# Odd layer of a two-block network: head scores as three fp32r products, and another spacing of the heads

## The chip, the cores and the metric

The kernel runs on one core of a Trainium2 chip. The metric is the device time of one execution in microseconds (us), median of several runs. Engines: PE is TensorE's matmul, PEld its weight load, DVE is VectorE, ACT is ScalarE, POOL is GpSimd, SP is SyncE.

## The reference, cut to what matters

Two blocks follow each other. The first has an even layer and an odd layer; the change touches the odd layer's mixer alone, an mLSTM with 8 heads over 256 latent and 256 context tokens. In short, for each head `h` and each direction `d` (causal and anti-causal):

```
D[q, k]  = i[k] + cum[q] - cum[k]           masked by the direction
mu[q]    = max_k D[q, k]
W_d[q,k] = (Q[q] . K[k]) / sqrt(128) * exp(D[q, k] - mu[q])
den[q]   = max(|sum_k W_d[q, k]|, exp(-mu[q] ...))
out[q]   = sum over d of (W_d / den) V ,  then gated, normalised per head, scaled
```

`Q` has 256 rows of 128 channels, `K` 512, `V` 512 rows of 256 channels. The normalisation of a head divides by the square root of the mean square of its 256 outputs. The outputs of all heads then go through the output weights.

## The kernel before

**How work is ordered.** Each engine runs one fixed instruction stream per layer. Every piece of work is a small generator that yields a due time, in an abstract unit, before each of its steps; `merge` takes the steps of all generators of an engine in the order of their due times (at equal due times in the order in which the stages are listed: `dense`, `heads`, `norm`, `turn`, `out`, and the weight feed last). So a due time does not start anything: it sets the place of an instruction in its engine's queue, and an instruction that waits holds up all behind it. ScalarE's table loads are put by the compiler in front of an ACTIVATE whose function the loaded table lacks.

**The stream of weights.** One unit of due time is 12 split matmuls of line 182 (`split_matmul`: lead x lead, lead x rest, rest x lead, each 128x512). The odd layer's input projection is four items of 16 units: v (units 16i to 16i+8, in four steps of 2), o (four steps of 1) and z (four steps of 1). In v a group of six matmuls is due every 0.5, in o and z too. For a step due at `u`, ACT takes the lead of the weights three steps ahead at `u + 0.02` (L343, after PE has finished the step before `u`), DVE takes the rest at `u + 0.3` (L155), and SP starts a load at `u + 0.5`. The output projection is units 64 to 80. The outputs of the groups are read by ACT: o with Sigmoid (L2634) at 16i+11.6 and 16i+12.1, z with Silu (L2624) at 16i+15.6 and 16i+16.1, v by ACT and DVE in turn (copies, L2616 and L2617).

**The heads.** Head `h` has a start `S`. Its steps and their due times, with `t` = 0, 1 the two blocks of 128 queries and `d` = 0, 1 the directions:

| engine | step (line) | due |
|---|---|---|
| DVE | maxima: decay tile and its row maximum (L2450, L2452) | S + 0.25 + d + 0.4t |
| ACT | decays: Exp of the tile, Exp of the floor (L2459, L2461) | S + 0.6 + d + 0.4t |
| PE | score (L2472) | S + 1.2 + 3t |
| DVE | mix: both directions times the score, sums, reciprocals (L2483 to L2492) | S + 2.2 + 3t |
| PE | four transposes of the mixed tile (L2503), wait for the mix | S + 3.6 + 3t |
| ACT | copy of the transposed tile (L2512) | S + 3.9 + 3t |
| PE | values (L2522) | S + 4.3 + 3t |
| DVE | gate (L2533) | S + 4.7 + 3t |
| ACT | Square with a sum (L2542) | S + 5.0 + 3t |
| DVE | gain times z, even heads (L2571) | S + 7.6 |
| DVE | mean (L2579), waits for the squares | S + 8.6 |
| ACT | Sqrt (L2587), waits for the mean | S + 8.7 |
| DVE | reciprocal and two scales (L2595, L2599), wait for the Sqrt | S + 9.1 |

The starts are 11.7, 17.7, 27.7, 33.7, 43.7, 49.7, 59.7 and 65.7. Behind the heads, `Turn` transposes the finished outputs of head `n` on PE (L783, one PSUM bank, so each waits for DVE's L2660 of the one before), ACT takes their lead (L2659) 0.3 later and DVE their rest (L2660) 0.6 later. The score is one fp32 matmul of 128x512, which the trace shows as two PE records. The keys `kT` and queries `qT` are fp32.

Of the kernel before, what the change touches and what calls it, by code (L numbers as in the profile page):

```python
# [7 lines left out]
ALU = mybir.AluOpType  # L8
# [5 lines left out]
P = 128  # L14
# [61 lines left out]
class Core:  # L76


    def __init__(self, nc, a, ctx):
        self.nc, self.a, self.ctx = nc, a, ctx  # L80
        sb = lambda name, shape: ctx.enter_context(nc.sbuf_tensor(name, shape, F32))
        with ExitStack() as c:
            low = lambda name, n, kind: c.enter_context(nc.sbuf_tensor(name, [P, n], kind))
            low("under_x", 2560, F32)
            first = low("q_lead0", BANK, F32R)
            low("under_ga", LEAD_GAP, F32)
            self.query_leads = (low("q_lead1", BANK, F32R), first)
        self.x = sb("x_res", [P, NT, D])
        self.hT = sb("hT", [P, KC, 2 * SEQ])
        self.ring = sb("weights", [P, Stream.RAW, 2048])  # L90
        self.cols = sb("cols", [P, NCOL])
        self.ident = sb("ident", [P, P])
        self.ga = sb("ga", [P, 3, D])
        self.mod = sb("mod", [P, 2, 2, KC, 2])
        self.gate = self.ga[:, 2, 0:72]
        self.gate_rows = nc.dram_tensor("gate_spread", (3 * KC, P), F32).ap()
        self.small = sb("small", [P, 256])
        self.ps = ctx.enter_context(nc.psum_tensor("psum", [P, 8, BANK], F32))
        keep = lambda name: ctx.enter_context(nc.semaphore(name))

        self.tables_in, self.tables_n = keep("tables_in"), 0
        self.stored = keep("result_stored")
        self.dve_chain = Chain(keep("dve_step"))
        self.act_chain = Chain(keep("act_step"))
        self.pool_chain = Chain(keep("pool_step"))
        self.stream = Stream(self, keep)
        self.fresh, self.old = ([], ExitStack()), ([], ExitStack())
# [293 lines left out]
class Feed(Stage):  # L401
# [19 lines left out]
    def leads(self, act):  # L421
        for i, at in self.ahead():
            yield at + self.offsets[0] + self.leads_later.get(i, 0.0)
            self.core.stream.take_lead(act, i)
# [4 lines left out]
    def rests(self, dve):  # L429
        if self.before:  # L430
            yield -2.0
            self.core.stream.take_rest(dve, self.before.last_split())
        for i, at in list(self.ahead())[:-1 if self.defer else None]:
            yield at + self.offsets[1] + self.rests_later.get(i, 0.0)
            self.core.stream.take_rest(dve, i)
# [1803 lines left out]
class OddRoom:  # L2239
    def __init__(self, core):  # L2240
        nc = core.nc
        sb = lambda s, name, shape: s.enter_context(nc.sbuf_tensor("o_" + name, shape, F32))
        with ExitStack() as c:
            v1 = sb(c, "v1", [P, NT, 2 * ML_V])
            with ExitStack() as early:
                self.v = (sb(early, "v0", [P, NT, 2 * ML_V]), v1)
                self.kT = sb(early, "kT", [P, ML_H, 2 * SEQ])
                self.h = Split(nc, early, "o_h", [P, KC, 2 * SEQ])
                self.o_gate = sb(early, "o", [P, LT, ML_H * ML_V])
                with ExitStack() as gates:  # L2250
                    self.wg = Split(nc, gates, "o_wg", [P, KC, P])
                self.Dm = sb(early, "decay", [P, LT, 2, 2 * SEQ])
                self.WT = sb(early, "WT", [P, LT, 2 * SEQ])
                self.spread = sb(early, "spread", [P, 2, 2 * SEQ])
            hs_first = c.enter_context(nc.sbuf_tensor("o_hs_first", [P, 8, SEQ], F32R))
            self.hsT = Split(nc, c, "o_hsT", [P, 16, SEQ])
        flat = core.hT[:].rearrange("p k t -> p (k t)")
        self.z = flat[:, 0:2048].rearrange("p (i t n) -> p i t n", i=2, t=LT)
        self.out_src = HeadFeatures(self.hsT, hs_first)
        self.gain = flat[:, 2048:3072].rearrange("p (i n) -> p i n", i=2)  # L2260
        self.scratch, self.wg32 = flat[0:40, 0:3072].rearrange("p (n t) -> p n t", n=6), flat[:, 3072:3712]
        self.junk = flat[:, 3712:3968]
        self.qT = core.ga[:, 0:2, :].rearrange("p a (b t) -> p (a b) t", t=SEQ)
        spare = core.x[:, LT:NT, :].rearrange("p t d -> p (t d)")
        self.masks = spare[:, 0:(2 * LT + 1) * SEQ].rearrange("p (n t) -> p n t", n=2 * LT + 1)
        self.aT = spare[0:40, 1280:1280 + 2 * SEQ]
        self.cumT = spare[:, 1792:1792 + LT * 40].rearrange("p (t r) -> p t r", t=LT)
        self.a_rows = nc.dram_tensor("gate_rows", (40, 2 * SEQ), F32).ap()
        self.mu, self.nmu, self.flr, self.den, self.rec = (core.small[:, 96 + 32 * i:128 + 32 * i] for i in range(5))
        self.ssq, self.root, self.norm = (core.small[:, 16 * i:16 * i + 16] for i in range(3))  # L2270
# [130 lines left out]
class Mlstm(Stage):  # L2401
# [3 lines left out]
    def __init__(self, core, odd, gates, dense, taps_done, banks, starts, step):  # L2405
        self.core, self.odd, self.gates, self.dense, self.taps_done, self.banks, self.starts, self.step = core, odd, gates, dense, taps_done, banks, starts, step
        s = lambda n: core.sem("ml_" + n)
        self.spread_in = [core.lasting(f"spread_in{i}") for i in range(2)]
        self.negmax, self.decayed, self.floored, self.scored = s("negmax"), s("decayed"), s("floored"), s("scored")
        self.mixed, self.turned, self.WT_ready, self.valued, self.out_done, self.squared = s("mixed"), s("turned"), s("WT_ready"), s("valued"), s("out_done"), s("squared")  # L2410
        self.tensor = (self.scores, self.turns, self.values)
        self.vector, self.scalar, self.gpsimd = (self.maxima, self.mixes, self.outs), (self.decays, self.copies, self.squares), (self.spreads,)

    def logs(self):

# [38 lines left out]
    def decays(self, act):  # L2454
        nc, odd = self.core.nc, self.odd
        for u, h, d, t, at in self.logs():
            yield at + 0.6
            act.wait_ge(self.negmax, u + 1)
            nc.scalar.activation(odd.Dm[:, t, d, :], odd.Dm[:, t, d, :], ACT.Exp, bias=odd.nmu[:, u:u + 1]).then_inc(self.decayed, 1)  # L2459
            r = 32 * d + h  # L2460
            nc.scalar.activation(odd.flr[:, u:u + 1], odd.cumT[:, t, r:r + 1], ACT.Exp, bias=odd.nmu[:, u:u + 1], scale=-1.0).then_inc(self.floored, 1)  # L2461

    def scores(self, pe):
        nc, ps, odd = self.core.nc, self.core.ps, self.odd
        for j, h, t, at in self.jobs(1.2):
            yield at
            if j == 0:
                pe.wait_ge(self.taps_done, 4)
                pe.wait_ge(self.gates.done, 1)
            else:  # L2470
                pe.wait_ge(self.mixed, j)
            nc.tensor.matmul(ps[:, self.banks[1], :], odd.qT[:, h, t * P:(t + 1) * P], odd.kT[:, h, :], start=True, stop=True).then_inc(self.scored, 1)  # L2472

    def mixes(self, dve):
        nc, ps, odd, link = self.core.nc, self.core.ps, self.odd, self.core.dve_chain
        for j, h, t, at in self.jobs(2.2):
            yield at
            dve.wait_ge(self.scored, j + 1)
            for d in range(2):
                u = 4 * h + 2 * d + t  # L2480
                c = slice(u, u + 1)
                dve.wait_ge(self.decayed, u + 1)
                link(dve, nc.vector.tensor_tensor_reduce(odd.Dm[:, t, d, :], ps[:, self.banks[1], :], odd.Dm[:, t, d, :],  # L2483
                                                         ML_QK ** -0.5, 0.0, ALU.mult, ALU.add, odd.den[:, c]))
            dve.wait_ge(self.floored, 4 * h + 2 + t + 1)
            both = lambda z: z[:, 4 * h + t:4 * h + t + 3:2]
            link(dve, nc.vector.scalar_tensor_tensor(out=both(odd.rec), in0=both(odd.den), scalar=-1.0, in1=both(odd.den), op0=ALU.mult, op1=ALU.max))
            link(dve, nc.vector.tensor_tensor(both(odd.den), both(odd.rec), both(odd.flr), ALU.max))
# [114 lines left out]
def odd_layer(core, odd):  # L2603
# [2 lines left out]
    keys_left = LeftOuts(core, "o_qk_left_", odd.qk, -4.0, 0.3)  # L2606
    gates.keys_out = keys_left.wait
    tokens = lambda n: [("tokens", t, 0, BANK) for t in range(n)]
    starts = [11.7 + 16 * (h // 2) + 6.0 * (h % 2) for h in range(ML_H)]
    taps_done = core.sem("taps_done")  # L2610

    def v_out(i, g):
# [41 lines left out]
    def turn_ready(pe, n):  # L2654
        pe.wait_ge(norm.scaled, 2 * n + 2)
        if n < 4:
            pe.wait_ge(heads.valued, 12)
    turn = Turn(core, "od_t_", blocks, [57.0, 58.2, 59.4, 60.6, 63.2, 63.9, 70.0, 76.0], (5,),
                act=lambda n: lambda act, src: nc.scalar.activation(hsT.lead(n), src, ACT.Copy),  # L2659
                dve=lambda n: lambda dve, src: nc.vector.tensor_tensor(hsT.rest(n), src, hsT.lead(n).bitcast(F32), ALU.subtract),  # L2660
                ready=turn_ready)
# [16 lines left out]
class OddEnd:  # L2678
# [5 lines left out]
    def tables_free(self, pool):  # L2684

        pool.wait_ge(self.heads.scored, LT * ML_H)
        pool.wait_ge(self.heads.floored, 2 * LT * ML_H)
        pool.wait_ge(self.heads.negmax, 2 * LT * ML_H)

    def x_ready(self, eng, k=KC - 1, t=LT - 1):  # L2690
# [969 lines left out]
```

## Time and profile before

| | |
|---|---|
| median of 3 runs | 1777.19 us (1777.16 to 1777.56) |
| profiled execution, its own time | 1777.32 us |
| its span in the trace | 1775.5 us |
| mean granted clock | 0.998 of full speed |
| PE busy | 1725.6 us (97%) |
| DVE busy | 1170.9 us (66%) |
| ACT busy | 917.4 us (52%) |
| odd layer's heads in the trace | about 664 to 890 us |

The span is what the trace holds from the first to the last instruction; the device time is 1.8 us longer in this execution. A matmul's end is modelled, so the cost of a matmul is read from one start to the next, not from its duration. In a timeline row the number in brackets is the engine's idle time before it, and what ended it.

### The profile page before, as it was taken

The numbers are of one execution on the slowest core, as the hardware profiler recorded it, in microseconds if no ns is written. First come the engines' busy times: TensorE is split into PE (matmuls) and PEld (weight loads), VectorE is DVE, ScalarE is ACT, GpSimd is POOL, SyncE is SP. The second block draws the span as 40 slices with busy tenths as digits, with TensorE's granted clock in tenths as the row PEclk, the third lists the DMA queues.
The fourth block names the chain that finished last, engine by engine and source line by source line (L and its number), as shares of the span: only waits on it lengthen the run. The fifth ranks groups of instructions, "written<-read, shape, count | busy, mean of one in ns | idle before, by whom it ended". The sixth has DMA issues, their size and how long they took to land. (4 is left out here: it accounts for less than half of the span.)

```text
span 1775.5 us, 22881 instructions
## 1 busy us (share of the span) xinstructions
PE 1725.6 (97%) x8547; PEld 1392.6 (78%) x8547; DVE 1170.9 (66%) x2154; ACT 917.4 (52%) x1497; POOL 49.5 (3%) x68
## 2 busy tenths in 40 slices
PE   8999999999998999999999999999999999999998
PEld 3866888777787777777778787788887787878886
DVE  6654566688438467766767775777646867577744
ACT  4332554433326355656656556467534746547743
POOL 0000000000000000000100002000000002000000
PEclk9999999999999999999999999999999999999999
DMA  9466221221325444453544444556555454555562
GB/s 344 152 207 214 96 72 48 72 72 56 134 95 191 138 125 127 149 154 110 164 154 149 143 155 166 171 182 193 190 190 159 137 165 142 184 165 178 190 217 74
DMA packets 115974, 267.24 MB, mean 151 GB/s; under 512 B 5413, under 2 KB 9838, under 8 KB 115673
## 3 DMA queue, kind: packets, MB, share of 16 engines
q1 hardware_dynamic: 111384, 252.26, 43.5%
q0 software_dynamic: 3504, 10.96, 2.1%
q10 hardware_dynamic: 976, 2.57, 0.4%
q8 instruction: 68, 1.11, 0.3%
q14 instruction: 42, 0.34, 0.1%
HBM read 264.63 MB, written 1.14 MB: 150 GB/s over the span
## 5 line engine op out<-in xcount | busy, mean ns | idle before, releaser
L155 DVE TENSOR_TENSOR qw_rest<-weights,qw_lead 128x1024 fp32r<-128x1024 f32 (+2 forms) x428 | 519.9, 1221 | 373.4 <-ACT qw_lead L343 368.1
L343 ACT ACTIVATE qw_lead<-weights 128x1024 fp32r<-128x1024 f32 (+2 forms) x428 | 446.2, 1048 | 454.1 <-PE psum L182 412.9
L182 PE MATMUL psum<-qw_lead,b_h_pair 128*128 128x512 f32 (+1 forms) x960 | 319.7, 398 | 4.0 <-ACT b_gates L3003 1.3
L182 PEld LDWEIGHTS psum<-qw_lead,b_h_pair 128*128 128x128 f32 x960 | 180.3, 188 | 44.7 <-issue 3.7
L182 PE MATMUL psum<-qw_rest,b_h_pair 128*128 128x512 f32 (+1 forms) x480 | 186.2, 388 | 0.0
L175 PE MATMUL psum<-b_h_pair,qw_lead 128*128 128x512 f32 x512 | 178.1, 393 | 2.0 <-DVE b_h_pair L722 2.0
L176 PE MATMUL psum<-b_h_pair,qw_rest 128*128 128x256 f32 x512 | 142.6, 279 | 0.0
L182 PE MATMUL psum<-e_h_lead,qw_lead 128*128 128x512 f32 x320 | 132.0, 413 | 2.2 <-DVE e_qT L1599 1.4
L182 PE MATMUL psum<-e_h_lead,qw_rest 128*128 128x512 f32 x320 | 125.7, 393 | 0.0
L182 PE MATMUL psum<-e_h_rest,qw_lead 128*128 128x512 f32 x320 | 125.0, 391 | 0.0
L175 PEld LDWEIGHTS psum<-b_h_pair,qw_lead 128*128 128x128 f32 x512 | 95.9, 187 | 24.3 <-DVE b_h_pair L722 2.8
L182 PE MATMUL psum<-qw_lead,o_h_lead 128*128 128x512 f32 x256 | 108.8, 425 | 0.3 <-PEq L129 0.3
L182 PEld LDWEIGHTS psum<-qw_rest,b_h_pair 128*128 128x128 f32 x480 | 90.4, 188 | 14.9
L182 PE MATMUL psum<-qw_lead,o_h_rest 128*128 128x512 f32 x256 | 100.0, 391 | 0.0
L182 PE MATMUL psum<-qw_rest,o_h_lead 128*128 128x512 f32 x256 | 99.9, 390 | 0.0
L182 PE MATMUL psum<-qw_lead,b_upT_rest 128*128 128x512 f32 x256 | 99.6, 389 | 0.0
L182 PE MATMUL psum<-qw_rest,b_upT_lead 128*128 128x512 f32 x256 | 99.6, 389 | 0.0
L182 PE MATMUL psum<-qw_lead,b_upT_lead 128*128 128x512 f32 x256 | 99.6, 389 | 0.0
L176 PEld LDWEIGHTS psum<-b_h_pair,qw_rest 128*128 128x128 f32 x512 | 96.5, 188 | 0.0
L182 PE MATMUL psum<-qw_lead,e_h_lead 128*128 128x512 f32 x224 | 88.6, 396 | 1.1 <-DVE e_qT L2149 1.1
L182 PE MATMUL psum<-qw_lead,e_h_rest 128*128 128x512 f32 x224 | 87.3, 390 | 0.0
L182 PE MATMUL psum<-qw_rest,e_h_lead 128*128 128x512 f32 x224 | 87.2, 389 | 0.0
(490 smaller groups left out, 3033.5 us busy)
## 6 DMA issues: line engine op xcount, KB each, us to landing
weights<-in_w_in SPq DMA_DIRECT2D x48, 1024.0 KB, 5.1
weights<-in_o_w_in SPq DMA_DIRECT2D x32, 1024.0 KB, 5.4
weights<-in_w_mlp_up SPq DMA_DIRECT2D x32, 1024.0 KB, 5.5
weights<-in_w_mlp_down SPq DMA_DIRECT2D x32, 1024.0 KB, 4.9
weights<-in_e_w_in SPq DMA_DIRECT2D x26, 1024.0 KB, 5.1
weights<-in_w_mod SPq DMA_DIRECT2D x24, 1024.0 KB, 7.2
weights<-in_e_w_out SPq DMA_DIRECT2D x8, 1024.0 KB, 5.0
weights<-in_o_w_out SPq DMA_DIRECT2D x8, 1024.0 KB, 4.9
```

What stands on the lines that cost most here:

```text
L155: return eng.tensor_tensor(self.rest[at], src, self.lead[at].bitcast(F32), ALU.subtract)
L175: nc.tensor.matmul(out, lhs[0], pair, start=start, stop=False)
L176: return nc.tensor.matmul(out[:, 0:lead.shape[1]], lhs[1], lead, start=False, stop=stop)
L182: mm = nc.tensor.matmul(out, l, r, start=start and i == 0, stop=stop and i == 2)
L343: self.core.nc.scalar.activation(self.buf.lead[self.at(u)], self.raw(u), ACT.Copy).then_inc(self.lead_ready, 1)
```

## The change

The score becomes three fp32r products of split heads, as everywhere else in the kernel. For that each head's `kT` (128x512) and `qT` (128x256) are split: ACT writes their leads (`leads`, due S - 0.95) and DVE subtracts them (`rests`, due S - 0.7), in place over `kT` and `qT`. PE waits for them at the score. The two semaphores of the decays become one. The starts become 11.7 + 7.7h (11.7, 19.4, 27.1, 34.8, 42.5, 50.2, 57.9, 65.6), and the first two output transposes are due 57.8 and 58.6 in place of 57.0 and 58.2. All other due times keep their distance from `S`.

```diff
+        with ExitStack() as c:
+            c.enter_context(nc.sbuf_tensor("under_hT", [P, 3072], F32))
+            self.odd_head_lead = c.enter_context(nc.sbuf_tensor("o_head_lead", [P, 3 * SEQ], F32R))
...
+            self.odd_q_rest = c.enter_context(nc.sbuf_tensor("o_q_rest", [P, ML_H, SEQ], F32R))
...
+                    self.k_rest = rests.enter_context(nc.sbuf_tensor("o_k_rest", [P, ML_H, 2 * SEQ], F32R))
...
-        self.junk = flat[:, 3712:3968]
+        self.junk = flat[:, 3840:4096]
+        self.k_lead, self.q_lead, self.q_rest = core.odd_head_lead[:, 0:2 * SEQ], core.odd_head_lead[:, 2 * SEQ:3 * SEQ], core.odd_q_rest
...
+        self.vector, self.scalar, self.gpsimd = (self.rests, self.maxima, self.mixes, self.outs), (self.leads, self.decays, self.copies, self.squares), (self.spreads,)
+
+    def leads(self, act):
+        odd = self.odd
+        for h in range(ML_H):
+            yield self.starts[h] - 0.95
+            if h:
+                act.wait_ge(self.scored, LT * h)
+                act.wait_ge(self.lead_then_rest, 4 * h)
+            else:
+                act.wait_ge(self.taps_done, 4)
+                act.wait_ge(self.gates.split, 4)
+            self.core.nc.scalar.activation(odd.k_lead, odd.kT[:, h, :], ACT.Copy).then_inc(self.lead_then_rest, 1)
+            self.core.nc.scalar.activation(odd.q_lead, odd.qT[:, h, :], ACT.Copy).then_inc(self.lead_then_rest, 1)
+
+    def rests(self, dve):
+        odd = self.odd
+        for h in range(ML_H):
+            yield self.starts[h] - 0.7
+            for rest, whole, lead in ((odd.k_rest, odd.kT, odd.k_lead), (odd.q_rest, odd.qT, odd.q_lead)):
+                dve.wait_ge(self.lead_then_rest, 4 * h + 2)
+                self.core.nc.vector.tensor_tensor(rest[:, h, :], whole[:, h, :], lead.bitcast(F32), ALU.subtract).then_inc(self.lead_then_rest, 1)
...
-            nc.tensor.matmul(ps[:, self.banks[1], :], odd.qT[:, h, t * P:(t + 1) * P], odd.kT[:, h, :], start=True, stop=True).then_inc(self.scored, 1)
+            if t == 0:
+                pe.wait_ge(self.lead_then_rest, 4 * h + 4)
+            qs = slice(t * P, (t + 1) * P)
+            split_matmul(nc, ps[:, self.banks[1], :], (odd.q_lead[:, qs], odd.q_rest[:, h, qs]), (odd.k_lead, odd.k_rest[:, h, :]), True, True).then_inc(self.scored, 1)
...
-                dve.wait_ge(self.decayed, u + 1)
+                dve.wait_ge(self.decay_then_floor, 2 * u + 1)
...
-            dve.wait_ge(self.floored, 4 * h + 2 + t + 1)
+            dve.wait_ge(self.decay_then_floor, 2 * (4 * h + 2 + t + 1))
...
-    starts = [11.7 + 16 * (h // 2) + 6.0 * (h % 2) for h in range(ML_H)]
+    starts = [11.7 + 7.7 * h for h in range(ML_H)]
...
-    turn = Turn(core, "od_t_", blocks, [57.0, 58.2, 59.4, 60.6, 63.2, 63.9, 70.0, 76.0], (5,),
+    turn = Turn(core, "od_t_", blocks, [57.8, 58.6, 59.4, 60.6, 63.2, 63.9, 70.0, 76.0], (5,),
```

## Rows read from the trace of the kernel before

**Rows 1.** The page: busy time, share of the span, instructions.

```profile
PE 1725.6 (97%) x8547; PEld 1392.6 (78%) x8547; DVE 1170.9 (66%) x2154; ACT 917.4 (52%) x1497; POOL 49.5 (3%) x68
```

**Rows 2.** Busy time of each engine in 30 us of the heads; last three: granted clock, DMA share, GB/s.

```profile
665.00:695.00 30.00, 29.26 (x128) 23.07 (x127) 22.47 (x56) 20.59 (x35) 2.68 (x5) 1.00 0.53 159
```

**Rows 3.** Waits of PE between 630 and 915 us: total, times, longest.

```profile
PE psum L2503 <- DVE o_decay L2492: 2.4, 4, 0.7
```

**Rows 4.** Timeline of PE around the first score.

```profile
666.82 1.02 PE L2472 MATMUL psum<-o_kT,ga 128*128 128x512 f32 x2
...
667.91 0.40 PE L182 MATMUL psum<-qw_rest,o_h_lead 128*128 128x512 f32 x1
```

**Rows 5.** Timeline of PE: the first head's transposes, then its values, then transposes unhindered.

```profile
674.30 0.39 PE L182 MATMUL psum<-qw_lead,o_h_rest 128*128 128x512 f32 x1
675.42 0.66 PE L2503 MATMUL psum<-ident,o_decay 128*128 128x128 f32 x4 [0.74 <-DVE o_decay L2492]
...
690.82 1.89 PE L2522 MATMUL psum<-o_v,o_WT 128*128 128x256 f32 x8
...
692.78 0.39 PE L182 MATMUL psum<-qw_rest,o_h_lead 128*128 128x512 f32 x1
...
698.00 0.60 PE L2503 MATMUL psum<-ident,o_decay 128*128 128x128 f32 x4
...
698.67 0.40 PE L182 MATMUL psum<-qw_rest,o_h_lead 128*128 128x512 f32 x1
```

**Rows 6.** Timeline of PE, late waits of the stage.

```profile
848.43 0.66 PE L2503 MATMUL psum<-ident,o_decay 128*128 128x128 f32 x4 [0.20 <-DVE o_decay L2492]
851.39 0.63 PE L783 MATMUL psum<-ident,o_o 128*128 128x128 f32 x4 [0.91 <-DVE o_hsT_rest L2660]
```

**Rows 7.** Timeline of ACT up to and through the first head's decays.

```profile
661.63 1.06 ACT L343 ACTIVATE qw_lead<-weights 128x1024 fp32r<-128x1024 f32 x1 [1.66 <-PE psum L182]
...
664.51 1.05 ACT L343 ACTIVATE qw_lead<-weights 128x1024 fp32r<-128x1024 f32 x1
665.45 0.59 ACT L2634 ACTIVATE o_o<-psum 128x512 f32<-128x512 f32 x1
666.06 1.28 ACT L2459 ACT_TABLE_LOAD   x1
667.35 0.72 ACT L2459 ACTIVATE o_decay<-o_decay,small 128x512 f32<-128x512 f32 x1
...
668.17 0.71 ACT L2459 ACTIVATE o_decay<-o_decay,small 128x512 f32<-128x512 f32 x1
```

**Rows 8.** Timeline of DVE: the first head's last maximum and mix.

```profile
671.19 0.68 DVE L2450 CUSTOM_DVE_ANT_0 o_decay<-o_spread,x_res 128x512 f32<-128x512 f32 x1
...
672.03 0.69 DVE L2483 CUSTOM_DVE_ANT_0 o_decay<-psum,o_decay 128x512 f32<-128x512 f32 x1
...
672.77 0.69 DVE L2483 CUSTOM_DVE_ANT_0 o_decay<-psum,o_decay 128x512 f32<-128x512 f32 x1
...
675.28 2.35 DVE L155 TENSOR_TENSOR qw_rest<-weights,qw_lead 128x1024 fp32r<-128x1024 f32 x2
```

**Rows 9.** Timeline of ACT: Exp's table loaded again behind a Sqrt, in a later layer.

```profile
960.72 1.28 ACT L3118 ACT_TABLE_LOAD   x1
...
963.21 1.28 ACT L2784 ACT_TABLE_LOAD   x1
```

**Rows 10.** Groups by line, 640 to 910 us: count, busy us, mean ns, idle before.

```profile
L2459 ACT ACT_TABLE_LOAD x8 | 10.3, 1283 | 0.1
L2599 DVE SCALAR_TENSOR_TENSOR o_o<-o_o,small,hT 128x256 f32<-128x256 f32 x16 | 7.0, 481 | 0.3
L2542 ACT ACTIVATE hT<-o_o 128x256 f32<-128x256 f32 x16 | 6.7, 416 | 22.9 <-DVE o_o L2533 22.9
...
L2587 ACT ACT_TABLE_LOAD x4 | 5.1, 1283 | 0.1
...
L2659 ACT ACTIVATE o_hsT_lead<-psum 128x512 fp32r<-128x512 f32 x8 | 4.7, 592 | 5.0 <-PE psum L783 5.0
```

More of the change, by code:

```diff
@@ L92, in __init__ @@
         self.ident = sb("ident", [P, P])
+        with ExitStack() as c:
+            self.odd_q_rest = c.enter_context(nc.sbuf_tensor("o_q_rest", [P, ML_H, SEQ], F32R))
         self.ga = sb("ga", [P, 3, D])
@@ L2246, in __init__ @@
                 self.v = (sb(early, "v0", [P, NT, 2 * ML_V]), v1)
+                with ExitStack() as rests:
+                    self.k_rest = rests.enter_context(nc.sbuf_tensor("o_k_rest", [P, ML_H, 2 * SEQ], F32R))
                 self.kT = sb(early, "kT", [P, ML_H, 2 * SEQ])
@@ L2408, in __init__ @@
         self.spread_in = [core.lasting(f"spread_in{i}") for i in range(2)]
-        self.negmax, self.decayed, self.floored, self.scored = s("negmax"), s("decayed"), s("floored"), s("scored")
+        self.negmax, self.decay_then_floor, self.lead_then_rest, self.scored = s("negmax"), s("decay_then_floor"), s("lead_then_rest"), s("scored")
         self.mixed, self.turned, self.WT_ready, self.valued, self.out_done, self.squared = s("mixed"), s("turned"), s("WT_ready"), s("valued"), s("out_done"), s("squared")
         self.tensor = (self.scores, self.turns, self.values)
-        self.vector, self.scalar, self.gpsimd = (self.maxima, self.mixes, self.outs), (self.decays, self.copies, self.squares), (self.spreads,)
+        self.vector, self.scalar, self.gpsimd = (self.rests, self.maxima, self.mixes, self.outs), (self.leads, self.decays, self.copies, self.squares), (self.spreads,)
[18 more added lines that the diff above has]
+                self.core.nc.vector.tensor_tensor(rest[:, h, :], whole[:, h, :], lead.bitcast(F32), ALU.subtract).then_inc(self.lead_then_rest, 1)
     def logs(self):
@@ L2458, in decays @@
             act.wait_ge(self.negmax, u + 1)
-            nc.scalar.activation(odd.Dm[:, t, d, :], odd.Dm[:, t, d, :], ACT.Exp, bias=odd.nmu[:, u:u + 1]).then_inc(self.decayed, 1)
+            nc.scalar.activation(odd.Dm[:, t, d, :], odd.Dm[:, t, d, :], ACT.Exp, bias=odd.nmu[:, u:u + 1]).then_inc(self.decay_then_floor, 1)
             r = 32 * d + h
-            nc.scalar.activation(odd.flr[:, u:u + 1], odd.cumT[:, t, r:r + 1], ACT.Exp, bias=odd.nmu[:, u:u + 1], scale=-1.0).then_inc(self.floored, 1)
+            nc.scalar.activation(odd.flr[:, u:u + 1], odd.cumT[:, t, r:r + 1], ACT.Exp, bias=odd.nmu[:, u:u + 1], scale=-1.0).then_inc(self.decay_then_floor, 1)
     def scores(self, pe):
@@ L2467, in scores @@
             if j == 0:
-                pe.wait_ge(self.taps_done, 4)
                 pe.wait_ge(self.gates.done, 1)
@@ L2686, in tables_free @@
         pool.wait_ge(self.heads.scored, LT * ML_H)
-        pool.wait_ge(self.heads.floored, 2 * LT * ML_H)
+        pool.wait_ge(self.heads.decay_then_floor, 4 * LT * ML_H)
         pool.wait_ge(self.heads.negmax, 2 * LT * ML_H)
```

## The prediction

> **What bounds the kernel now.** I read the page first: PE is busy 97% of the span [rows 1], and in 30 us of the heads it works 29.3 us at the full granted clock while DVE works 22.5 and ACT 20.6 [rows 2]. So the layer costs what PE's queue costs plus the places where PE waits. Next the waits of PE from 630 to 915 us: the only one that repeats is the head's transposes (L2503) waiting for DVE's mix, four times, 2.4 us by the records [rows 3]. Then the timeline of PE, because ends are modelled there and only starts can be trusted. Between 692.78 and 698.00 there are 23 split matmuls, 0.227 us each [rows 5]. A group of six is therefore 1.36 us, a unit of due time 2.72. By starts the first head's transposes begin 675.42 and could have begun 674.30 + 0.23 = 674.53: 0.9 us lost, and so in the first head of the second and third pair. The fourth loses 0.4 at 848.43, L783 at 851.39 loses 1.1, having waited for L2660 of the transposes before it [rows 6], and one of its kind 0.2: 4.4 us in all. Last the timelines of ACT and DVE before the first mix, to see what made it late: ACT loads a table and works off Sigmoid, Exp and the weight lead in turn [rows 7], and DVE's last maximum, ahead of the mix in its queue, stands behind a weight rest that waited for such a lead [rows 8]. The feed of split weights itself never holds PE up for long. That is the reader's picture: PE has no slack, and between a head's score and its transposes lie 2.4 units in which ACT and DVE must get through.
>
> **What PE saves.** A score goes from 666.82 to 667.91 - 0.23, so 0.86 us [rows 4]. Three split products of the same shape cost 3 x 0.227 = 0.68. For 16 scores that is 16 x 0.18 = 2.9 us. Both bounds: the three could cost more where they meet other work, the first matmul behind transposes starting late (698.67 against 698.00 makes transposes cost 0.44, [rows 5]), but the score has split matmuls before and behind it nearly everywhere, so I take 2.9, with 0 as the other end.
>
> **What is added.** The trace has no split of a head. Nearest are the fp32r copy of 128x512, 0.59, and an ACTIVATE of 128x256, 0.42 [rows 10], so about 1.0 us of ACT for each head and, since L155 takes 1.17 for 1024 columns [rows 8], about 1.1 of DVE. They are due 2.1 units (5.8 us) ahead of the score. For the first head they fall where ACT has 1.66 us idle [rows 7]; I price them at nothing there. Without such cover they delay the decays by up to 1.0 a head, which I count for the last head alone, where the gains precede them.
>
> **What the spacing moves.** This is the larger part. A head's Sqrt is due S + 8.7. With starts 7.7 apart that is the next head's S + 1.0, the very due time of its second Exp, with two more Exp behind. Before, the next start was S + 6 or S + 10, and the Sqrt fell behind all four Exp or ahead of them. A Sqrt between Exps needs a table load before and after it: the trace shows Exp's table loaded again right behind Sqrt's at 963.21 [rows 9], 1.28 us each. Beside it, the Trainium skill (ScalarE: Activation LUTs, section "Table sets: the hidden batching unit") says that calls should be batched by set, all Exps and then all Sqrts, since the two lie in different sets; this change does the opposite. The same page (section "What ACT_TABLE_LOAD costs") gives about 2.66 us for each switch with a drain; here Exp starts 1.29 after its load began and the load began as the Sigmoid ended, so the trace does not agree, and by that figure each load below would cost 1.4 more. Also, the Sigmoids of o (16i + 11.6, 16i + 12.1) no longer precede the Exps of heads 2, 4 and 6 but fall among them.
>
> By the due times head 2 gets: Sigmoid 27.6, Exp 27.7, weight lead 28.02, Sigmoid 28.1, Exp 28.1, Sqrt 28.1, Exp 28.7. That is six table loads where the first head of a pair had two. Counting the whole stage, about 13 loads are added, 16.7 us of ACT. The prices: load 1.29, Exp with floor 0.82, weight lead 0.94, Sigmoid 0.6 (starts in [rows 7]), Square with its read 0.5 and Sqrt 0.2 (a little above [rows 10] and from the same timeline as [rows 9]), mix 3.25 of which 2.51 after its second operand, from DVE to PE 0.14 [rows 5, 8]. From PE to ACT I take 0.2.
>
> Head 2, from the end of the values of head 1 (PE at 27.0): 0.2 + 0.94 + Square 0.5 + (1.29 + 0.6) + (1.29 + 0.82) + 0.94 + (1.29 + 0.6) + (1.29 + 0.82) + Sqrt (1.29 + 0.2) + (1.29 + 0.72) + mix 2.51 + 0.14 = 16.7 us. PE in that time has four units and a score, 4 x 2.72 + 0.68 = 11.6. It waits 5.2 us.
>
> Head 4 starts with Exp's table loaded: from 43.0, 0.2 + 0.94 + 0.82 + 0.82 + Sqrt 1.49 + Sigmoid 1.89 + 0.94 + 0.6 + 2.01 + 2.51 + 0.14 = 12.4 against seven groups and a score, 10.2: 2.2 us.
>
> Head 5, from the values' end at 50: 0.2 + 0.94 + 0.5 + 1.29 + 0.82 + 0.82 + 1.49 + 2.11 + lead 0.94 + rest 1.17 (due 52.3, just ahead of the mix at 52.4) + 3.25 + 0.14 = 13.7 against eight groups and a score, 11.6: 2.1 us. Heads 1 and 3 have the same Exp, Sqrt, Exp. There DVE's scales wait for the Sqrt and the last maximum stands behind them: for head 1, gate 0.6, Square 0.5, 2.11, lead 0.94, 0.82, 1.49, scales 1.0 (two of 0.48, [rows 10]), maximum 0.84, 3.25, 0.14 = 11.7, so 0.1 lost; for head 3 a rest more but less waiting for ACT, 11.9, so 0.3.
>
> Head 6: its Exps share ACT with Sqrt, both Sigmoids and the copies of the output transposes. The third copy, due 59.7, stands behind Exp, copy, Exp, Sqrt, lead, Exp and Sigmoid. From 58.0 it ends at 12.0 us, its rest on DVE at 12.7; PE reaches the fourth output transposes (60.6) at 10.0: 2.7 us. Behind it 0.4 at the values of head 6, whose copy follows the second Sigmoid, and 1.2 at the transposes due 63.9, where 1.1 was lost before. Head 7: the gains hold DVE until 1.6 after the values, then Square, lead, 2.11, 0.82, 1.49, lead, scales, maximum, rest and mix: 14.0 against 11.6, 2.4 us. Head 0 keeps its old order and its old mix time, but PE arrives 0.18 earlier: 1.1.
>
> **The sum.** Waits after: 1.1 + 0.1 + 5.2 + 0.3 + 2.2 + 2.1 + 2.7 + 0.4 + 1.2 + 2.4 = 17.7 us; before: 4.4. Less 2.9 for the scores: 17.7 - 4.4 - 2.9 = 10.4 us more. The profiled execution took 1777.3 us (span 1775.5), 0.1 above the median, so I predict 1787.7 us. Nothing after the heads changes its order: the last transposes stay at 76.0 and the output units at 64 to 80. The values (1.73, [rows 5]) and transposes cost what they did. No weight rest comes later than some 3 us before PE needs it, so the feed itself costs nothing.
>
> **Rivals.** (1) Faster: the even spacing does what even spacing should. For it speaks that ACT is idle a third of the time [rows 2] and that the mixes' waits came in the first heads of pairs only. If the table loads were covered, the waits beyond head 0's would go: -2.9 - 4.4 + 1.1 = -6.2, 1771. It decides if the 2.4 units (7.2 us with the score) suffice, that is if no head's ACT work runs beyond the 11.6 us window worked out above. Against it: head 2's loads alone are 7.7 us. Chance 0.14. (2) Nearly no change: heads 2 and 4 wait as computed, the others, computed within 3 us of their windows, do not: 7.4 + 1.1 + 1.1 (at 63.9) - 4.4 - 2.9 = +2.3, and a little more cover brings it within 0.2% (3.6 us): about 1779. Chance 0.12. (3) Dearer: queues fall so far behind that split weights arrive late too, or the clock falls when PE stands for 5 us. The rest due 29.3 ends about 18 us after 27.0 and PE needs it at 32, some 4.5 us later, after its own wait; five late rests of 1.2 us would add 6: 1794. PE's clock stood at 1.00 in every stretch I read, but no wait in them was as long. Chance 0.08. The forecast has 0.66. (4) That the change doesn't act: only if the scores cost 0.86 still; it takes 2.9 off the gain and leaves the sign.
>
> **Range and chances.** The low end joins rivals 1 and 2 at 1776, the high end 1794 is rival 3; about 1 in 10 lies below and less above. Forecast and rival 3, and a little of rival 2, are slower by over 0.2% (3.6 us, about what a measurement can tell): 0.77. Within 0.2%: 0.10. Faster: 0.13.
>
> **What would show it.** Right: some 33 table loads between 640 and 910 us in place of 20; PE waiting before the third head's transposes by about 5 us; L2503's waits for DVE the largest of PE's; three matmuls of 0.23 for a score. Wrong: L2503 without waits, or loads not placed between Exp and Sqrt. The likeliest error is the order at equal due times (28.1, 44.1), where another order of Sigmoid and Exp saves a load or two, and the 0.2 us steps that add up along ten instructions.

## The result, and the profile after

The changed kernel takes 1792.7 us (median of five, 1792.3 to 1798.2) against 1777.2 for the kernel before: ratio 1.0093, 95% interval 1.0080 to 1.0106, 15.6 us more. The profiled execution spans 1790.9 us, 15.4 more than before.

The page's line of busy times. PE and DVE have hardly more to do, ACT has 23 us more than its 917.4 in [rows 1]:

```profile
PE 1727.3 (96%) x8563; PEld 1400.0 (78%) x8563; DVE 1177.7 (66%) x2170; ACT 940.5 (53%) x1526; POOL 49.4 (3%) x68
```

Groups of ACT between 640 and 925 us, the table loads. There are 34 of them; before there were 21, with Exp's 8 and Sqrt's 4 in [rows 10]. L2488 is the Exp of the decays, L2618 the heads' Sqrt, L2665 the Sigmoid, L2655 the Silu. Line numbers are those of the changed kernel.

```profile
L2488 ACT ACT_TABLE_LOAD x15 | 19.2, 1283 | 0.3
L2618 ACT ACT_TABLE_LOAD x8 | 10.3, 1283 | 0.1
L2665 ACT ACT_TABLE_LOAD x6 | 7.7, 1283 | 0.1
L2655 ACT ACT_TABLE_LOAD x4 | 5.1, 1283 | 0.1
L2393 ACT ACT_TABLE_LOAD x1 | 1.3, 1283 | 0.0
```

Waits of PE from 630 to 930 us: engine, line, who it waited for, total, times, longest. The transposes' wait for the mix (L2534, L2503 before) went from 2.4 us in four to 14.3 in seven [rows 3]:

```profile
PE psum L2534 <- DVE o_decay L2523: 14.3, 7, 5.4
PE psum L788 <- DVE o_hs_first L2691: 2.8, 1, 2.8
PE psum L788 <- DVE o_hsT_rest L2691: 1.1, 1, 1.1
```

Timeline of PE at the first score: three matmuls from 665.42 to 666.11, 0.69 us in place of 0.86 [rows 4].

```profile
665.42 0.39 PE L187 MATMUL psum<-o_head_lead 128*128 128x512 f32 x1
665.65 0.39 PE L187 MATMUL psum<-o_k_rest,o_head_lead 128*128 128x512 f32 x1
665.88 0.40 PE L187 MATMUL psum<-o_head_lead,o_q_rest 128*128 128x512 f32 x1
666.11 0.40 PE L187 MATMUL psum<-qw_lead,o_h_lead 128*128 128x512 f32 x1
```

Timeline of ACT before the third head's mix. Read it from top to bottom: Sigmoid, Exp, weight lead, Sigmoid, Exp, Sqrt, Exp, each but the weight lead behind a load of 1.28, with no idle time between them.

```profile
718.08 1.28 ACT L2665 ACT_TABLE_LOAD   x1
719.38 0.60 ACT L2665 ACTIVATE o_o<-psum 128x512 f32<-128x512 f32 x1
720.00 1.28 ACT L2488 ACT_TABLE_LOAD   x1
...
722.10 1.05 ACT L348 ACTIVATE qw_lead<-weights 128x1024 fp32r<-128x1024 f32 x1
723.17 1.28 ACT L2665 ACT_TABLE_LOAD   x1
...
725.08 1.28 ACT L2488 ACT_TABLE_LOAD   x1
...
727.30 1.28 ACT L2618 ACT_TABLE_LOAD   x1
...
728.82 1.28 ACT L2488 ACT_TABLE_LOAD   x1
730.11 0.72 ACT L2488 ACTIVATE o_decay<-o_decay,small 128x512 f32<-128x512 f32 x1
```

Timeline of DVE in the same place: it stands 3.6 us at the reciprocal that waits for the Sqrt, with the last maximum and the mix queued behind it.

```profile
728.83 0.17 DVE L2626 RECIPROCAL small<-small 128x2 f32<-128x2 f32 x1 [3.62 <-ACT small L2618]
...
729.83 0.69 DVE L2479 CUSTOM_DVE_ANT_0 o_decay<-o_spread,x_res 128x512 f32<-128x512 f32 x1
...
730.68 0.69 DVE L2514 CUSTOM_DVE_ANT_0 o_decay<-psum,o_decay 128x512 f32<-128x512 f32 x1
...
733.27 0.75 DVE L2523 SCALAR_TENSOR_TENSOR o_decay<-o_decay,small 128x512 f32<-128x512 f32 x1
```

Timeline of PE there. It stands from 728.53 to 734.07, 5.5 us, and then the split matmuls come 0.43 apart, not 0.227, until 738.

```profile
728.30 0.39 PE L187 MATMUL psum<-qw_lead,o_h_rest 128*128 128x512 f32 x1
734.07 1.12 PE L2534 MATMUL psum<-ident,o_decay 128*128 128x128 f32 x4 [5.39 <-DVE o_decay L2523]
734.84 0.78 PE L187 MATMUL psum<-qw_lead,o_h_lead 128*128 128x512 f32 x1
735.41 0.63 PE L187 MATMUL psum<-qw_rest,o_h_lead 128*128 128x512 f32 x1
735.84 0.63 PE L187 MATMUL psum<-qw_lead,o_h_rest 128*128 128x512 f32 x1
...
738.34 0.40 PE L187 MATMUL psum<-o_head_lead,o_q_rest 128*128 128x512 f32 x1
```

Busy times in stretches; the third number from the end is the granted clock as a share of 2.4 GHz. It was partly at the lower level, 1.2 GHz, behind the wait.

```profile
700.00:730.00 30.00, 28.52 (x129) 23.08 (x127) 18.51 (x42) 20.77 (x29) 0.71 (x2) 1.00 0.45 137
730.00:735.00 5.00, 0.93 (x5) 0.93 (x6) 4.76 (x13) 3.70 (x7) 0.54 (x1) 0.64 0.17 52
735.00:740.00 5.00, 5.00 (x17) 4.09 (x17) 2.51 (x3) 3.42 (x4) 0.00 (x0) 0.67 0.53 141
```

**Where the 15.4 us are.** From the first score to the next layer's first matmul the trace of before takes 246.8 us (666.82 to 913.60), that of after 262.7 (665.42 to 928.15): 15.9 more. Ahead of it the execution before lost 1.4 us to a lower clock at 355 to 365 us that the one after did not have, behind it the one after lost 0.9. Within the stretch: waits counted by starts 19.6 against 4.4, +15.2; scores -2.9; matmuls at the lower clock after the waits at 734 (2.0) and 852 (1.3), +3.3. The clock was low at 926 too, on the last transposes of the stretch, but there it costs 0.1 only: they take 2.37 us to the next matmul against 2.27 before, because the kernel before waited for DVE in the same place, 0.5 us in all. That makes 15.7 for 15.9.

Timeline of PE at the end of the stretch, the kernel before:

```profile
911.33 1.09 PE L701 MATMUL psum<-ident,x_res 128*128 128x128 f32 x8 [0.61 <-DVE x_res L1889]
...
913.60 0.50 PE L182 MATMUL psum<-qw_lead,b_h_pair 128*128 128x512 f32 x1 [0.23 <-DVE b_h_pair L722]
```

The changed kernel:

```profile
925.78 2.45 PE L706 MATMUL psum<-ident,x_res 128*128 128x128 f32 x11 [0.61 <-DVE x_res L1894]
...
928.15 0.79 PE L187 MATMUL psum<-qw_lead,b_h_pair 128*128 128x512 f32 x1
```

### The profile page after: what moved, and what is told of

It is laid out like the page before. It is cut to its first block and busy times, and to the rows that moved or that the text cites. A ratio compares the mean times of both kernels' runs of the same rounds, so it can differ in the third digit from the quotient of the medians.

```text
span 1790.9 us, 22973 instructions
## 1 busy us (share of the span) xinstructions
PE 1727.3 (96%) x8563; PEld 1400.0 (78%) x8563; DVE 1177.7 (66%) x2170; ACT 940.5 (53%) x1526; POOL 49.4 (3%) x68
## 5 line engine op out<-in xcount | busy, mean ns | idle before, releaser
L160 DVE TENSOR_TENSOR qw_rest<-weights,qw_lead 128x1024 fp32r<-128x1024 f32 (+2 forms) x428 | 520.0, 1222 | 356.1 <-ACT qw_lead L348 350.8
L187 PE MATMUL psum<-qw_lead,o_h_lead 128*128 128x512 f32 x256 | 105.0, 410 | 0.3 <-PEq L134 0.3
```

The lines of the kernel that those rows point to most:

```text
L160: return eng.tensor_tensor(self.rest[at], src, self.lead[at].bitcast(F32), ALU.subtract)
L187: mm = nc.tensor.matmul(out, l, r, start=start and i == 0, stop=stop and i == 2)
```

## The experiments

The ratios are against the kernel before, run on the same chip in the same session; its median was between 1777.4 and 1778.2. "Stretch" is the time from the first score to the next layer's first matmul in the profiled execution, 246.8 us before and 262.7 after.

### The split alone

```diff
-    starts = [11.7 + 7.7 * h for h in range(ML_H)]
+    starts = [11.7 + 16 * (h // 2) + 6.0 * (h % 2) for h in range(ML_H)]
...
-    turn = Turn(core, "od_t_", blocks, [57.8, 58.6, 59.4, 60.6, 63.2, 63.9, 70.0, 76.0], (5,),
+    turn = Turn(core, "od_t_", blocks, [57.0, 58.2, 59.4, 60.6, 63.2, 63.9, 70.0, 76.0], (5,),
```

> The changed kernel with the old starts and the old output transposes: the split of the heads and the three products alone. If the order of ACT's queue is the cause, this gains what the scores save, 2.9 us, less 0.2 at each of the four or five places where PE already waited for a mix: 1774.5 to 1775.5, some 20 table loads between 640 and 910 us, no wait of PE over 1.3 us. If the added leads and rests (1.0 us of ACT and 1.1 of DVE a head) are the cause, it is slower than before, 1780 or more, and L2534's waits grow.

Measured 1777.1 us, ratio 0.9999 (0.9990 to 1.0008): no change, and less of a gain than either 2.9 or the 2 expected. Table loads are 21 again. Waits of PE in its trace, 630 to 900 us:

```profile
PE psum L2534 <- DVE o_decay L2523: 4.5, 4, 1.6
PE psum L788 <- DVE o_hsT_rest L2691: 0.9, 1, 0.9
```

The stretch is 246.3 us, 0.5 less. By starts the four waits at the mixes are 1.2, 1.1, 1.7 and 1.3, 5.3 us where the kernel before had 3.1: the scores' gain is spent on waiting, 0.18 a time because PE is earlier, and most of the rest because the leads and rests push the mix back at the fifth and seventh head. At the fifth ACT works without a break from the leads at 773.37 to the Exp at 779.90, so the leads' 0.8 us delay all behind them. The forecast had counted such a delay for the last head alone. The clock was low again from 910 to 915, but it costs nothing before the stretch ends: the last transposes take 2.28 us to the next matmul, 2.27 before. So the split doesn't cause the loss; nor does it gain.

### The spacing alone

```diff
-    starts = [11.7 + 16 * (h // 2) + 6.0 * (h % 2) for h in range(ML_H)]
+    starts = [11.7 + 7.7 * h for h in range(ML_H)]
...
-    turn = Turn(core, "od_t_", blocks, [57.0, 58.2, 59.4, 60.6, 63.2, 63.9, 70.0, 76.0], (5,),
+    turn = Turn(core, "od_t_", blocks, [57.8, 58.6, 59.4, 60.6, 63.2, 63.9, 70.0, 76.0], (5,),
```

> The kernel before with the even starts and the new output transposes: one fp32 score of 0.86 us, no split. If the order is the cause, it shows all the waits of the changed kernel, each 0.2 shorter since PE arrives later, and pays 2.9 for the scores: 1793 to 1795, 33 table loads, the third head's wait 5.3 us and the clock's fall behind it. If the split is the cause, 1777 to 1780.

Measured 1794.2 us, ratio 1.0088 (1.0075 to 1.0102), with the same 34 loads. Its waits of PE:

```profile
PE psum L2503 <- DVE o_decay L2492: 12.8, 6, 5.2
PE psum L783 <- DVE o_hs_first L2660: 2.6, 1, 2.6
PE psum L783 <- DVE o_hsT_rest L2660: 1.1, 1, 1.1
```

The third head's 5.2 us against 5.4 with the split, and the granted clock at 0.50 from 735 to 740 us behind it. This is what was expected if the order is the cause. The whole loss comes with the starts (the first two output transposes moved with them).

### Without the loads for the Sqrt

```diff
-            self.core.nc.scalar.activation(odd.root[:, c], odd.root[:, c], ACT.Sqrt).then_inc(self.rooted, 1)
+            self.core.nc.scalar.activation(odd.root[:, c], odd.root[:, c], ACT.Identity).then_inc(self.rooted, 1)
```

> The changed kernel with Identity in place of the heads' Sqrt (the head norms are not the reference's): the same instructions in the same order, without the table loads around the Sqrt. If the loads are the cause, the waits fall to about 1.2 (first head), 3.0 (third), 1.1 (fifth), 0.4 and 1.3 at the output transposes, 7 us in place of 19.6, and perhaps one slow stretch of PE is left: 1776 to 1779. If it is the place of the Sqrt in the queue (its wait for the mean, the scales waiting for it) or the spacing as such, 1789 to 1793.

Measured 1783.0 us, ratio 1.0025 (1.0016 to 1.0034), between the two ranges expected. The profiled execution was 1779.7, one of two with a mean granted clock of 0.999; the seven at 0.993 to 0.996 took 1782.7 to 1784.9. The stretch is 250.9 us, 11.8 less. Loads fall to 20 in the heads, the Ln's included. The direction is as expected, the size is not: at the third head 4.1 us by starts (4.0 by the record) are left, not 3.0.

```profile
PE psum L2534 <- DVE o_decay L2523: 7.2, 5, 4.0
PE psum L788 <- DVE o_hsT_rest L2691: 1.1, 1, 1.1
```

The timelines tell why: ACT's Identity starts at 726.70, but only behind the loads for Sigmoid and Exp ahead of it, and DVE's scales, last maximum and mix run off one after the other from there, so the load saved behind the Identity no longer counts.

```profile
726.92 0.17 DVE L2626 RECIPROCAL small<-small 128x2 f32<-128x2 f32 x1 [2.20 <-ACT small L2618]
...
728.77 0.69 DVE L2514 CUSTOM_DVE_ANT_0 o_decay<-psum,o_decay 128x512 f32<-128x512 f32 x1
```

### Without the loads for Sqrt and Sigmoid

```diff
-                          act=lambda g, cs=cs: lambda act, src: nc.scalar.activation(odd.o_gate[:, g, cs], src, ACT.Sigmoid)))
+                          act=lambda g, cs=cs: lambda act, src: nc.scalar.activation(odd.o_gate[:, g, cs], src, ACT.Identity)))
```

beside the edit of the run before.

> As the run with Identity for Sqrt, and Identity for the Sigmoid of the o gates too (neither is the reference's). If the loads are the cause, only the first head's wait and the one at the sixth output transposes stay, 2.5 us: 1771 to 1773, below the kernel before, with the granted clock at 1.00 throughout. If the even spacing itself or the split costs time, it stays above 1777.

Measured 1772.8 us, ratio 0.9974 (0.9963 to 0.9984), stretch 243.6. Even spacing, split, every instruction and every wait in its old place, and 10 loads in the heads: with the loads gone, the loss is gone. That is fewer than the 21 of the kernel before, so part of the gain over it is not the layout's. The waits are 3.2 us by the records and not 2.5, for the eighth head waits too.

```profile
PE psum L2534 <- DVE o_decay L2523: 2.1, 3, 1.1
PE psum L788 <- DVE o_hsT_rest L2691: 1.1, 1, 1.1
```

### The Sqrt behind the next head's Exps

```diff
-    norm = HeadNorm(core, odd, heads, dense, [at + 8.6 for at in starts])
+    norm = HeadNorm(core, odd, heads, dense, [at + (10.4 if h < ML_H - 1 else 8.6) for h, at in enumerate(starts)])
```

> The changed kernel, output as the reference's, with the head norms' mean, Sqrt and scales due 1.8 later for all but the last head, so behind the next head's four Exp. By the loads and the queue: third head 2.4, fifth 0.7, first 1.2, sixth output transposes 1.2, others nothing, 5.5 us in place of 19.6 and less of the slow clock: 1775 to 1778. If the even spacing costs by itself, above 1785.

Measured 1787.1 us, ratio 1.0050 (1.0034 to 1.0066): my size was wrong. The stretch is 254.5, 8.2 less than after. The third head waits 2.2 by starts, as expected, but the fifth still 2.3: I had forgotten that the moved Sqrt leaves its table loaded, so the fifth head's first Exp, which found its own before, must load one. 29 loads remain in the heads, the Ln's included. A wait of the values for ACT's copy is new:

```profile
PE psum L2534 <- DVE o_decay L2523: 7.1, 6, 2.1
PE psum L2553 <- ACT o_WT L2543: 1.8, 1, 1.8
PE psum L788 <- DVE o_hsT_rest L2691: 1.1, 1, 1.1
```

The eighth head waits 1.5. By its own words the expectation had read a time above 1785 as a cost of the even spacing by itself. The run before speaks against that reading: it has the same spacing without the loads and takes 1772.8.

The clock fell behind waits of 2.2 and 2.3 us:

```profile
730.00:735.00 5.00, 2.99 (x11) 2.26 (x10) 4.52 (x13) 4.22 (x7) 0.00 (x0) 0.77 0.54 156
...
790.00:795.00 5.00, 4.37 (x14) 3.65 (x15) 3.87 (x7) 3.34 (x5) 0.00 (x0) 0.66 0.25 94
```

### An even layout with the tables in order

```diff
-    starts = [11.7 + 7.7 * h for h in range(ML_H)]
+    starts = [11.7, 19.7, 27.7, 35.7, 43.7, 51.7, 59.7, 65.9]
...
-    norm = HeadNorm(core, odd, heads, dense, [at + 8.6 for at in starts])
+    norm = HeadNorm(core, odd, heads, dense, [at + (10.4 if h < ML_H - 2 else 8.6) for h, at in enumerate(starts)])
...
-    turn = Turn(core, "od_t_", blocks, [57.8, 58.6, 59.4, 60.6, 63.2, 63.9, 70.0, 76.0], (5,),
+    turn = Turn(core, "od_t_", blocks, [59.1, 60.0, 60.9, 61.8, 63.2, 63.9, 70.0, 76.0], (5,),
```

with the later transposes of the next run.

> Split, starts 8.0 apart (11.7 to 59.7, the last 65.9), norms behind the next head's Exps, the o gates' Sigmoids ahead of the Exps, first transposes 0.5 later, the first four output transposes moved behind the sixth head's values. Even layout without the interleaved tables: if the order on ACT was all, no wait over 0.5 us but the one at the output transposes due 63.9 (1.2 us), 1771 to 1773. If an even layout costs DVE or PE something else, 1776 or more.

Measured 1777.4 us, ratio 0.9999 (0.9990 to 1.0007), stretch 246.5. No mix is waited for any more, but the output transposes, closer together in the one bank, wait 3.2 us for DVE, and the values 2.0 for ACT's copy:

```profile
PE psum L788 <- DVE o_hs_first L2691: 3.2, 3, 2.1
PE psum L2553 <- ACT o_WT L2543: 2.0, 3, 0.7
```

So the second half of the expectation came true: this even layout costs something else, at the output transposes and at the copies, with 24 loads in the heads. An even layout needn't lose 15 us, but this one gains nothing over pairs.

### Later transposes, with the split and without

```diff
         for j, h, t, at in self.jobs(3.6):
-            yield at
+            yield at + (0.5 if t == 0 else 0.0)
...
         for j, h, t, at in self.jobs(3.9):
-            yield at
+            yield at + (0.3 if t == 0 else 0.0)
```

> Split and three products, old starts, and the transposes of each head's first block due 0.5 later (their copy 0.3). In the run with the split alone PE waited 1.2, 1.1, 1.7 and 1.3 us at those transposes. If these waits are where the scores' 2.9 us went, PE now does a group of split matmuls (1.36 us) in their place, some 5 us are gained and the time is 1772 to 1773.5. If PE's arrival was not what made them, or the later transposes delay the values, it stays at 1776 to 1778.

> The kernel before with the same later transposes and nothing else. PE waited 0.9, 0.9, 0.9 and 0.4 us there: 1774 to 1775.5. Beside the run with split and later transposes it shows what the three products are worth when no wait takes it back: 2.9 us if the price by starts is right, nothing if the split's work costs as much elsewhere.

Measured 1775.9 us with the split and the old starts (0.9987, 0.9978 to 0.9996), 1775.7 without the split (0.9984, 0.9975 to 0.9992). The waits at the mixes are gone but for 0.2. Without the split the expected gain is nearly there; with it, it fell short by 2 to 4 us, and the stretch is 244.1 against 243.9. Part of it went to the wait of the sixth output transposes for the rest of the fifth, 2.1 us by the record against 1.4:

```profile
PE psum L788 <- DVE o_hsT_rest L2691: 2.1, 1, 2.1
```

The clock was below full speed behind it, where the values take 2.6 us to the next matmul (849.02 to 851.64) in place of 1.5, and again at 905 to 915 us.

### And the sixth output transposes later

```diff
-    turn = Turn(core, "od_t_", blocks, [57.0, 58.2, 59.4, 60.6, 63.2, 63.9, 70.0, 76.0], (5,),
+    turn = Turn(core, "od_t_", blocks, [57.0, 58.2, 59.4, 60.6, 63.2, 65.1, 70.0, 76.0], (5,),
```

> The run with split, old starts and later transposes, and the sixth output transposes (due 63.9, where PE waited 2.4 us for DVE's rest of the fifth) due 65.1. If that wait is the last one in the heads' stretch, it goes, and the slow clock behind it: from the first score to the next layer's first matmul 241 us or less in place of 244.1, 1772 to 1774 in time. If the wait only moves to another transpose, 1775 to 1776.

> The same without the split, on the kernel before with later transposes, where that wait was 1.7 us: 1774 to 1775. The difference of the two stretches in the trace is what the three products are worth when nobody waits: 2.9 us if the price of 0.86 against 0.68 holds.

Measured 1774.1 us with the split (0.9978, 0.9968 to 0.9988) and 1774.0 without it (0.9974, 0.9964 to 0.9984). Both beat both kernels of this study. The stretches are 241.6 and 243.2: 1.6 us for the three products, not 2.9. By starts the trace with the split waits 1.4 us (0.4 for a mix, 1.1 for ACT's copy) against 0.7, so some 2.4 us come from PE's work itself. The clock was low at 905 to 910 with the split and full without, but up to the end of the stretch this costs nothing (the last transposes take 2.28 us in both). In the times nothing of the gain is seen.

```profile
PE psum L2553 <- ACT o_WT L2543: 0.9, 1, 0.9
PE psum L2534 <- DVE o_decay L2523: 0.2, 1, 0.2
```

## Why the prediction was right, and where it was off

The forecast was slower by 10.4 us, the kernel is slower by 15.6, inside the range.

**The order on ACT.** This held, for the third head instruction by instruction. Predicted were the six loads before the third head's mix and some 33 in place of 20 in the heads; the trace has 33, and one Ln load in both kernels. With the loads taken out of an otherwise unchanged queue the loss vanished, and with the starts alone it came whole. The Trainium skill (ScalarE: Activation LUTs, section "Table sets: the hidden batching unit") says to batch calls by set; the runs agree. Its 2.66 us for a switch (section "What ACT_TABLE_LOAD costs") does not fit: in the trace above each load took 1.28, as the page has it, but the next ACTIVATE began 1.29 to 1.30 after the load did.

**The waits, one by one** (predicted, then by starts in the trace): first head 1.1, 1.2; second 0.1, 0.3; third 5.2, 5.5; fourth 0.3, 1.3; fifth 2.2, 2.4; sixth 2.1, 2.0; fourth output transposes 2.7, 3.0; values of the seventh head 0.4, none; sixth output transposes 1.2, 1.3; eighth head 2.4, 2.6. Sum 17.7, 19.6. The fourth head's was the one mis-sized: the gains (L2602), due just ahead of the gate, ran until 751.7 behind a weight rest and held the gate for 0.8 us (it began 2.7 us after its values did, unhindered ones 1.9); I had counted that for the last head only.

**The scores.** 0.69 for 0.86 is as predicted, 0.17 each. But "less 2.9" as a net term was too simple where a wait follows: in the run with the split alone it bought 0.5 us of the stretch. In the changed kernel it does count, since the waits above already hold PE's earlier arrival.

**The clock.** Here the sum failed. It had no term for it; rival 3 named the clock falling where PE stands some 5 us, with a chance of 0.08. It fell, also behind the 3.0 us wait at the output transposes, and cost 3.4 us of the profiled stretch. With 1.9 us of waits beyond the forecast and 0.9 of low clock later, less the 1.4 that the execution before lost at 355 to 365 us, that is 4.8 of the 5.0 us by which the difference of the spans, 15.4, lies above 10.4. That the result is still inside the range is partly luck: the upper end, 1794, was worked out from five late weight rests, 6 us, which did not come.

**The rivals.** That even spacing would bring the expected evenness (1771) fell with the first trace, though the run without the loads, 1772.8, shows what it would have been. Late weight rests, the other half of rival 3, did not come: PE never waited for L160 in the stretch. Rival 2, that only the third and the fifth head lose time, fell too: the sixth and the eighth head and the fourth output transposes waited 2.0, 2.6 and 3.0 us.

## What to carry to other kernels

In a hand-ordered queue, moving one group of steps moves its functions among those of its neighbours: list the functions of ScalarE in their new order and count the table changes ahead of the step that PE waits for, and remember which table the last one leaves behind. A cheaper matmul in front of a wait that another engine ends is worth little (here 0.5 of 2.9 us); give PE other work until the wait is over (here one group of matmuls ahead of a later transpose), with the cheaper matmul or without: that gained 1.5 us or more in four runs. A wait of a few microseconds of the engine that bounds the kernel can cost more than its length, since the clock may fall behind it (3.4 us beside 19.6 of waits here).

## What the runs showed of the hardware

In these traces the granted clock fell to the lower of its two levels behind some waits of PE and not behind others: behind 5.5, 5.3 and 4.1 us at the same place in three kernels, also behind 2.2 and 2.3 us in one run, but not behind 2.4 and 2.6 us in the changed kernel's own trace; and behind 3.0 us at the fourth output transposes there, but not behind 2.8 us at the same place with the spacing alone. Which short waits are hit differs from execution to execution: the kernel before had a slow stretch at 355 us, its later relatives at 560, 910 or 1340 us. That shows in the times: over all executions of the kernel before, those with a mean granted clock of 0.999 have a median of 1775.8 us, of 0.998 1777.2, of 0.997 1778.1, of 0.996 1779.9 (and the few of 0.995 1779.1); single executions leave this order, one of 0.999 took 1782.1. Differences of 1 to 2 us, such as what the split is worth, lie within that, and the runs here don't settle them. In the last two runs the executions with the split are some 2 us shorter at the same mean clock (1772.1 and 1772.3 at 0.997 against 1774.0 to 1775.0), but four of eight had only 0.994 or 0.995, and none of the nine without it. With later transposes alone it was 8 of 11 against 2 of 11; with the split alone, 1 of 11. Why the split kernels with later transposes more often had the lower clock stays open, and equal means prove little, since a low clock where PE would wait anyway cost nothing (the end of the stretch, in the run with the split alone).
